# Expert slots in another order, and a norm that feeds the router tile by tile

## The reference

```
h = rmsnorm(x, norm2_g) * (1 + sc2) + sh2            # sc2, sh2: one row per request
g_prob = softmax(h @ w_grp + b_grp)                  # 4 groups, the best one is taken
e_prob = softmax((h @ w_rt + b_rt)[group])           # 8 experts of that group, the best two
weights = g_top * e_top / sum(e_top)
hid = silu(h @ w_gate[e]) * (h @ w_up[e])            # 32 experts, 1024 -> 256
x = x + g2 * sum over both experts of weights * (hid @ w_down[e])     # 256 -> 1024
```

## Time and profile before

| | |
|---|---|
| median of 3 runs | 2094.83 us (2093.8 to 2096.57) |
| the profiled execution's own time | 2091.81 us |
| its span, first to last instruction | 2090.0 us |
| PE busy | 1800.3 us (86%) |
| DVE busy | 759.5 us (36%) |
| ACT busy | 349.6 us (17%) |
| DMA, mean over the span | 211 GB/s, 441.07 MB |
| TensorE clock, mean granted | 0.927 of full speed |

### The profile page before, as it was taken

One profiled execution on the slowest core, in us unless ns is written; L12 is line 12 of the kernel. 1 busy time (PEld: TensorE's weight loads), 2 busy tenths in 40 slices (PEclk: granted clock), 3 DMA queues, 4 the chain that ended last, 5 costly groups with the idle time before them and its releaser, 6 DMA issues. The chain is left out here.

```text
span 2090.0 us, 22577 instructions
## 1 busy us (share of the span) xinstructions
PE 1800.3 (86%) x8114; PEld 1065.3 (51%) x8114; DVE 759.5 (36%) x1560; ACT 349.6 (17%) x524; POOL 75.2 (4%) x73
## 2 busy tenths in 40 slices
PE   4999999889879959988479999998897897798883
PEld 2666657556447634333136666574574565443321
DVE  2153256656223242211324233565732242331113
ACT  1013112232110021111001222121420201111000
POOL 0000000000000001110000000000000000111100
PEclk8999999989999969999789999998999999799996
DMA  7565422324475628999376653324146673499972
GB/s 296 182 233 192 141 81 89 118 82 142 150 238 222 279 81 359 423 422 413 108 271 213 216 169 123 102 72 147 57 132 200 236 298 145 151 422 423 424 313 77
DMA packets 107128, 441.07 MB, mean 211 GB/s; under 512 B 19394, under 2 KB 54498, under 8 KB 79746
## 3 DMA queue, kind: packets, MB, share of 16 engines
q1 hardware_dynamic: 79442, 408.63, 51.9%
q10 hardware_dynamic: 18352, 20.40, 3.1%
q0 software_dynamic: 9216, 10.51, 1.5%
HBM read 433.70 MB, written 28.84 MB: 221 GB/s over the span
## 5 line engine op out<-in xcount | busy, mean ns | idle before, releaser
L364 PE MATMUL ps<-s_proj_and_h,w_in_tiles 128*128 128x320 f32 x1280 | 354.5, 438 | 8.3 <-PEq L203 8.3
L364 PEld LDWEIGHTS ps<-s_proj_and_h,w_in_tiles 128*128 128x128 f32 x1280 | 243.9, 192 | 123.5 <-issue 26.9
L177 PE MATMUL ps<-s_proj_and_h,w_in_tiles 128*128 128x320 f32 x960 | 294.5, 456 | 7.3 <-PEq L1178 6.1
L2056 PE MATMUL ps<-s_proj_and_h,t_ex_xf 128*64 128x512 f32 x1024 | 245.2, 634 | 35.3 <-DMA s_proj_and_h<-w_gate_up 33.7
L177 PEld LDWEIGHTS ps<-s_proj_and_h,w_in_tiles 128*128 128x128 f32 x960 | 186.1, 200 | 96.3 <-issue 35.5
L2056 PEld LDWEIGHTS ps<-s_proj_and_h,t_ex_xf 128*64 128x64 f32 x1024 | 82.9, 146 | 194.0 <-issue 194.0
L1760 PE MATMUL ps<-s_proj_and_h,w_merge 128*128 128x320 f32 x512 | 140.0, 436 | 3.8 <-PEq L1670 3.8
L1760 PEld LDWEIGHTS ps<-s_proj_and_h,w_merge 128*128 128x128 f32 x512 | 98.0, 192 | 45.9 <-issue 6.2
L2080 PE MATMUL ps<-w_down_slots,t_ex_hf 128*64 128x512 f32 x512 | 116.9, 598 | 2.5 <-DVE t_ex_hf L2127 1.0
L2125 DVE TENSOR_TENSOR t_ex_hid<-t_ex_hid,ps 128x256 f32<-128x256 f32 x32 | 13.5, 421 | 258.4 <-ACT t_ex_hid L2151 258.4
L1765 PE MATMUL ps<-s_proj_and_h,w_merge 128*128 128x320 f32 x256 | 71.3, 433 | 2.6 <-issue 2.6
(11 more groups left out here) (427 smaller groups left out, 1981.9 us busy)
## 6 DMA issues: line engine op xcount, KB each, us to landing
s_proj_and_h<-w_gate_up SPq DMA_DIRECT2D x64, 2048.0 KB, 25.0
w_in_tiles<-w_in SPq DMA_DIRECT2D x140, 512.0 KB, 3.6
w_down_slots<-w_down SPq DMA_DIRECT2D x64, 1024.0 KB, 25.6
w_mod_panels<-w_mod SPq DMA_DIRECT2D x32, 1024.0 KB, 7.4
page_keys<-pages_k SPq DMA_DIRECT2D x128, 192.0 KB, 3.3
s_proj_and_h<-w_mod SPq DMA_DIRECT2D x16, 1024.0 KB, 11.8
w_merge<-w_branch SPq DMA_DIRECT2D x16, 1024.0 KB, 5.0
page_values<-pages_v ACTq DMA_DIRECT2D x96, 128.0 KB, 3.1
```

The source lines that it names most:

```text
L177: mm = pe.matmul(K.ps[:, self.BANKS[i % 2], 0:T], self.win[:, j, k, :], K.h[:, k, :], start=(k == 0), stop=(k == KD - 1))
L364: mm = pe.matmul(K.ps[:, n % BANKS, 0:T], win[:, j, k, :], K.h[:, k, :], start=(k == 0), stop=(k == KD - 1))
L2056: mm = pe.matmul(K.ps[rows, GU, :], xf[:, k, rows], K.gate_up[:, j, k, :], start=(k == 0), stop=(k == KD - 1))
```

## The change

The norm gets a stage of its own that works in tile pairs and holds the router's products. The ACT table for the root is asked for inside the merge, by a root of one element. The places get a semaphore apart from the counts. The constant `K.slot` becomes a permutation: place n gets slot 8 (n mod 8) + (n + n/8) mod 8.

```diff
+def router_norm_stage(K, R):
+        def _(act):
+            act.wait_ge(s("n2_sum"), 1)
+            root_of_mean(K, rstd[:, :], K.ps[:, 0, 0:T], D).then_inc(s("n2_root"), 1)
+            for k in range(KD):
+                act.wait_ge(s("n2_scaled"), k // 2 + 1)
+                nc.scalar.activation(K.h[:, k, 0:SEQ], K.h[:, k, 0:SEQ], ACT.Identity, scale=K.gain[:, 1, k, 0:1],
+                                     bias=K.mod[:, 24 + k, 0:1]).then_inc(s("n2_prompt"), 1)
...
+            def scale(i):
+                v.tensor_tensor(K.h[:, 2 * i:2 * i + 2, :], K.x[:, 2 * i:2 * i + 2, :],
+                                rstd[:, :].unsqueeze(1).to_broadcast([P, 2, T]), ALU.mult).then_inc(s("n2_scaled"), 1)
+            def samples(i, op, a):
+                h = sample(K.h[:, 2 * i:2 * i + 2, :])
+                return v.tensor_tensor(h, h, a[:, :, 1:NREQ].unsqueeze(3).to_broadcast([P, 2, NB, TS]), op)
+            dve.wait_ge(s("n2_root"), 1)
+            link(v.reciprocal(rstd[:, :], rstd[:, :]))
+            scale(0)
+            for i in range(KD // 2):
+                if i + 1 < KD // 2:
+                    scale(i + 1)
+                dve.wait_ge(s("n2_scaled"), i + 1)
+                link(samples(i, ALU.mult, K.gain[:, 1, 2 * i:2 * i + 2, :]))
+                samples(i, ALU.add, K.mod[:, 24 + 2 * i:26 + 2 * i, :]).then_inc(s("n2_samples"), 1)
...
+            pe.wait_ge(s("rt_w_loaded"), 16)
+            for k in range(KD):
+                pe.wait_ge(s("n2_prompt"), k + 1)
+                pe.wait_ge(s("n2_samples"), k // 2 + 1)
+                mm = pe.matmul(K.ps[0:36, 1, 0:T], R.w_router[:, k, :], K.h[:, k, :], start=(k == 0), stop=(k == KD - 1))
+            mm.then_inc(s("rt_products"), 1)
 # merge_stage, ACT, after the last square
+            act.wait_ge(s("n2_added"), 3)
+            nc.scalar.activation(squares[:, 2, 0:1], K.eps[:, 0:1], ACT.Sqrt)
 # router_stage, PE: the products are gone; after the last product for the places
+            mm.then_inc(s("rt_places"), 1)
 # router_stage, DVE
-            dve.wait_ge(s("rt_counts"), 1)
             link(v.memset(R.pos[:, :, :], -1.0))
+            dve.wait_ge(s("rt_places"), 1)
...
+            dve.wait_ge(s("rt_counts"), 1)
             link(v.tensor_reduce(total[:, 0:1], K.ps[0:1, 3, 0:NEXP], AX.X, ALU.max))
 # constants
-    slot = np.tile(np.arange(CAP, dtype=f), (P, 1))
+    n = np.arange(CAP)
+    slot = np.tile(np.argsort(8 * (n % 8) + (n + n // 8) % 8).astype(f), (P, 1))
```

More of the change, by code:

```diff
@@ L273, in sum_over_partitions, with _ @@
     return mm
+def router_norm_stage(K, R):
+    nc, s = K.nc, K.sem
+    with nc.sbuf_tensor("n2_rstd_row", [P, T], F32) as rstd, nc.Block(no_gpsimd_drain=True) as block:
+        @block.scalar
+        def _(act):
[5 more added lines that the diff above has]
+                                     bias=K.mod[:, 24 + k, 0:1]).then_inc(s("n2_prompt"), 1)
+        @block.vector
+        def _(dve):
+            v, link = nc.vector, lambda ins: K.vc.link(dve, ins)
+            def scale(i):
[13 more added lines that the diff above has]
+                samples(i, ALU.add, K.mod[:, 24 + 2 * i:26 + 2 * i, :]).then_inc(s("n2_samples"), 1)
+        @block.tensor
+        def _(pe):
+            pe.wait_ge(s("rt_w_loaded"), 16)
[4 more added lines that the diff above has]
+            mm.then_inc(s("rt_products"), 1)
 def norm_stage(K, n, tag):
@@ L1821, in router_stage @@
         sb = lambda n, sh: e.enter_context(nc.sbuf_tensor("t_" + n, sh, F32))
-        w, bias = R.w_router, R.b_router
+        bias = R.b_router
         L, g = sb("rt_L", [P, 3, 36]), sb("rt_g", [P, 4, 3, 4])
@@ L1837, in _ @@
         def _(pe):
-            pe.wait_ge(s("rt_w_loaded"), 16)
             def turn_h(r):
@@ L1846, in turn_h @@
                 mm.then_inc(s("h_tm"), 1)
-            for k in range(KD):
-                mm = pe.matmul(K.ps[0:36, 0, 0:T], w[:, k, :], K.h[:, k, :], start=(k == 0), stop=(k == KD - 1))
-            mm.then_inc(s("rt_products"), 1)
             turn_h(0)
@@ L1853, in _ @@
             for r, (t0, n) in enumerate(REG):
-                mm = pe.transpose(K.ps[0:n, 1, r * 36:(r + 1) * 36], LT[:, t0:t0 + n], K.ident[0:36, 0:36])
+                mm = pe.transpose(K.ps[0:n, 0, r * 36:(r + 1) * 36], LT[:, t0:t0 + n], K.ident[0:36, 0:36])
             mm.then_inc(s("rt_logits"), 1)
@@ L1862, in _ @@
                     pe.matmul(K.ps[0:n, 2, r * NEXP:(r + 1) * NEXP], K.ones[:, 0:n], sel[:, 2, q, :], start=(q == 0), stop=False)
-                pe.matmul(K.ps[0:n, 2, r * NEXP:(r + 1) * NEXP], K.causal[0:n, 0:n], sel[0:n, 2, r, :], start=(r == 0), stop=True)
+                mm = pe.matmul(K.ps[0:n, 2, r * NEXP:(r + 1) * NEXP], K.causal[0:n, 0:n], sel[0:n, 2, r, :], start=(r == 0), stop=True)
+            mm.then_inc(s("rt_places"), 1)
             for r, (t0, n) in enumerate(REG):
@@ L1884, in _ @@
             dve.wait_ge(s("rt_logits"), 1)
-            v.tensor_copy(L[:, 0:2].rearrange("p r c -> p (r c)"), K.ps[:, 1, 0:72])
-            link(v.tensor_copy(L[0:NSAMP, 2], K.ps[0:NSAMP, 1, 72:108]))
+            v.tensor_copy(L[:, 0:2].rearrange("p r c -> p (r c)"), K.ps[:, 0, 0:72])
+            link(v.tensor_copy(L[0:NSAMP, 2], K.ps[0:NSAMP, 0, 72:108]))
             G, E = L[:, :, 0:4], L[:, :, 4:36].rearrange("p r (g e) -> p r g e", g=4)
@@ L1932, in _ @@
             act.wait_ge(s("rt_products"), 1)
-            nc.scalar.activation(LT[:, :], K.ps[0:36, 0, 0:T], ACT.Identity, bias=bias[:, 0:1]).then_inc(s("rt_biased"), 1)
+            nc.scalar.activation(LT[:, :], K.ps[0:36, 1, 0:T], ACT.Identity, bias=bias[:, 0:1]).then_inc(s("rt_biased"), 1)
             for r, (t0, n) in enumerate(REG):
@@ L2326, in build @@
                     merge_stage(K, l, wb, R)
-                norm_stage(K, 1, "n2")
+                router_norm_stage(K, R)
                 R.hT = e.enter_context(nc.sbuf_tensor("rt_h_tm", [P, 3, D], F32))
```

## The result

The changed kernel takes 2064.4 us (median of 4 runs, 2061.83 to 2069.34), the kernel before in the same session 2095.7 (2093.8 to 2096.66): ratio 0.9855, 95% interval 0.9833 to 0.9876. Run again in a later session it took 2068.59 (2063.35 to 2069.36) against 2096.26: 0.9863 (0.9837 to 0.9889).

The account below looks back on a forecast made before the run. The DMA engines bound the expert stage, so whatever ends earlier ahead of it moves it one for one. Slots, scatters, norm and products, and places sum to 11.3 us a layer, 22.6 off 2094.83: 2072 us, within 2063 to 2084.

Parts of the forecast that it names:

- The slots: End of the expert weight stream: rows spread evenly over DMA engines, so PE's last pair starts 6.3 and 6.6 us earlier.
- The 1.9 us left for unevenness: Expert stream's end: deducted from at most 8.2 and 8.5 us for the level load's own end and whole rows.
- The first rival: Expert stream: rows are dealt around the engines whatever their slot, so 9.0 us remain, 2086; chance 0.12.
- spread rows get dearer: Gathers and scatters: spread rows cost more than 182 ns each, making the kernel slower, 2104 at 200 ns more; chance 0.04.
- The last scatters: Scatters at the expert stages' ends, alone on the DMA engines: 0.5 us saved in the first layer, 0.2 in the second.
- Norm and products: Between merge and router: PE sets the pace without gaps and the logits' transposes come 3.8 us earlier a layer.
- The bound from above: Norm and products: with full clock at once, DVE's last samples at 746.6 us bound, and 5.2 us comes out.
- The early table: Merge's end: ACT loads the root's table right behind the last square, so the root ends 0.5 us earlier.
- The rival of cold products: Router products: PE waits tile by tile and never regains its clock, 1.2 us instead of 3.8, 2077; chance 0.15.
- Places: DVE's step behind the places: clearing moves ahead of the wait, 0.7 us a layer, between 0.3 and 0.9.
- The sum: Whole kernel: 11.3 us in each layer, 22.6 us in all.
- more than the sum: Rival: the stream's end quite level and PE's clock back early, 1.9 + 1.4 us more a layer, 2066; chance 0.07.

Follow-up runs that it names:

- experiment 4: Changed kernel with eight successive places put in two groups of four slots, 32 apart: 2105.41 us, ratio 1.0048 to the kernel before.
- experiment 3: Changed kernel with the slot order lacking its rotation inside the blocks of eight: 2085.57 us, ratio 0.9954 to the kernel before.
- experiment 1: Kernel before with the new order of slots alone: 2078.32 us against 2095.11, ratio 0.9915.
- experiment 10: Changed kernel with eight unused float32 products on PE in the norm, ahead of its first wait: 2072.55 us, ratio 0.9885 to the kernel before.
- experiment 6: Changed kernel without the small root in the merge, so the root's table loads in the norm: 2067.64 us, ratio 0.9864 to the kernel before.
- Experiment 5: Kernel before with only the places' own semaphore and the clearing ahead of the wait: 2093.2 us against 2096.8, ratio 0.9983.
- experiment 7: Changed kernel with 14 unused float32 products on PE in the norm, ahead of its first wait: 2079.38 us, ratio 0.9922 to the kernel before.
- experiment 9: Changed kernel run again unaltered, in a later session: 2068.59 us against 2096.26 for the kernel before, ratio 0.9863.
- experiment 11: Changed kernel with unused products on PE, eight in the norm, seven behind the third block's transposes, five ahead of the first gather: 2062.81 us, ratio 0.9834 to the kernel before.

## Why the prediction was right

**The slots** (forecast 6.3 and 6.6, measured 6.12 and 7.05; alone 5.95 and 7.23). The step held in cause and size: the rows of a list fell on few engines, and a load counts as landed with its slowest engine. The 1.9 us left for unevenness were taken and not worked out; the count of experiment 4 gives 2.0 and 1.9. Experiments 3 and 4 show it from the other side, since two other orders of the same rows and bytes lose the gain or cost 23 us. The first rival, that the slots change nothing, is refuted by experiment 1; that spread rows get dearer, by the 182 ns of the kernel after.

The Trainium skill, "DMA: Bandwidth & Descriptors", The descriptor swizzle, gives engine by partition in groups of four, two of them 32 apart, for a transfer to 128 partitions. No row named an engine before; the runs agree with it for these gathers and scatters by rows: eight packets at a time at 198 to 225 GB/s in experiment 3, and 18 us lost in each layer in experiment 4.

**The last scatters** (forecast 0.5 and 0.2, measured 0.32 and 0.10): right in kind, too small to matter.

**Norm and products** (forecast 3.8 a layer, measured 3.78 and 3.64). PE started 5.96 us behind the squares, forecast 6.2, and set the pace as forecast; its run took 7.23 us instead of 6.70, since more of it lay at the low clock: 5.61 us busy at 0.50, against 4.58 at 0.51. Transposes at 14.61, forecast 14.5. The bound from above, 5.2, was too low: it puts DVE's last samples 10.4 us behind the squares (746.6), since it counts one of the four multiplies twice, and they ended 8.87 behind (746.60 after 737.73). In experiment 10, with the clock up, the transposes came 6.1 and 5.6 us earlier than in the kernel before. The early table (0.5 in the sum) moved the root by 0.7 us; experiment 6, without it, loses that much at the transposes in one layer and nothing in the other, and its time cannot be told from the changed kernel's. The rival of cold products is out: the granted clock rose to 1.00 within the run and `turn_h(0)` took 1.06 us.

On the rule of the Trainium skill, "ScalarE: Activation LUTs", What ACT_TABLE_LOAD costs, 2.66 us with a drain: here a load takes 1.28 us and the next root starts at once behind it, in the norm too (738.36 behind 737.07 + 1.28), so no drain is seen in these rows.

**Places** (forecast 0.7 a layer, measured 0.84 and 0.75; alone 0.63 and 0.84): right.

**The sum.** The four steps measure 13.17 + 0.42 + 7.42 + 1.59 = 22.6 us, as forecast. That the sum agrees to the tenth is luck: its parts miss by up to 0.18 us one way and 0.45 the other, and the misses cancel. The time fell by more, 25.6 in the profiled executions and 27.7 to 31.3 in the medians. What was left out of the sum:

- The first gate-up of each layer, costed at nothing. In the two kernels without the places' edit it took 9.80 to 9.91 us in all four layers; in the seven kernels with it and no unused products (14 layers) 8.40 to 9.86, 8.93 on average, so some 0.9 us a layer. Experiment 5 has it with the places alone. But three of the 14 lie at 9.78 to 9.86, and in experiments 7 and 10, which have the edit and unused products in the norm, it took 9.44 to 9.91: the shorter gate-up mostly goes with the edit, and that the edit is its cause is not shown. The granted clock of that stretch was 0.71 before and 0.81 after; a gate-up wholly at full clock takes 7.09. Why the clock is back earlier in some executions stays open.
- The final norm, 24.19 us in the profile of before, took 21.8 to 23.0 in the twelve others, experiment 1 among them, which leaves it as it was: that execution was an odd one, not a gain.
- Against that, the end of the squares came 1.77 us later, in stretches that the change hardly touches. Over the thirteen profiles it lay at 733.8 to 742.6 us in the first layer and 726.3 to 732.8 in the second.

With the first gate-ups the sum is 24.4. The interval of the first comparison is 26.0 to 35.0 us, that of the second 23.3 to 34.2; what is left up to the medians' 27.7 and 31.3, 3 to 7 us, these runs don't place. The rival "more than the sum" named the right end of the range and the wrong reasons: a quite level end was not there (the slots gave their 13.2), and neither did the clock come back early in the products.

## What to carry to other kernels

Where an indirect DMA moves only some rows of a tile, the rows' places in the tile choose the DMA engines, and a stream of large loads beside it ends with the busiest engine: look at how the tenths die away at the end of a stream, and spread short lists over groups of four partitions, not over larger blocks. A stretch of DMA-bound work is moved one for one by what stands ahead of it, so the gaps of the other engines there are worth their full length. Unused products that raise PE's clock have to be weighed against the real product that they hold up. Here 14 in a gap of 5.96 us cost more than they gave; eight, seven and five in three gaps gave 2.8 and 2.5 us by layer in the traces, although the eight ended after the first tile was ready, and no time clear of noise. Count two MATMULs for each float32 product.

## What the runs showed of the hardware

- Half of the 16 engines carried 198 to 225 GB/s for some 15 us in experiment 3, half of the 423 of all of them: an engine's rate didn't rise when the others stopped.
- In the last scatter of the kernel before, a packet of a 4 KB row took 159 ns and one of 4 bytes 9 ns; there were 57 of the first kind and 87 of the second, with 71 empty slots.
- The same eight unused products after the same work ran at a granted clock of 1.00 in experiment 10 (4.54 us) and of 0.72 in experiment 11 (6.24 us), each about 1.0 us after PE's last squares, and the 14 of experiment 7 took 7.78 us in one layer and 9.46 in the other: whether the clock falls there is not fixed by the program's order.
- A single packet of instructions during a read-back went with an end 1.3 to 3.4 us longer than in experiment 9 in both layers of experiment 10; that it did so by chance isn't excluded.
